# Gate broadcast, head squares and convolution steps of an mLSTM layer reordered and recast in a three-layer kernel

## The chip, the cores and the metric

One core of one Trainium2 chip runs the whole program in one launch. The metric is the device time of one execution in microseconds, as the median of several runs. TensorE (PE) multiplies, VectorE (DVE) and ScalarE (ACT) do the elementwise work, and SyncE (SP) issues the DMAs of the weights. GpSimd has almost nothing to do.

## The reference, cut to what matters

The kernel computes a block of multi-head latent attention, a block of mLSTM and a third block of mixed attentions with a large feed-forward part, for 256 tokens of width 2048 in float32. The change lies in the mLSTM block only. For each of its 8 heads (dk = 128, dv = 256), with `T` = 256 tokens:

```python
qk = silu(causal_depthwise_conv(x @ W_qk, w, b))       # 4 taps, 16 blocks of 128 rows
i, f = split(x @ W_g + gate_b)                         # 8 heads each
lf = log_sigmoid(f);  F = cumsum(lf)                   # over the tokens
a = i - F;            M = cummax(a)
D[s, t] = exp(a[s] - M[t])  for s <= t
A = (k^T q) * dk**-0.5 * D
h = (A^T v) / max(|sum_s A|, exp(-M - F))
h = rmsnorm(h) * head_norm;   out = (h * sigmoid(o) * silu(z)) @ W_out
```

The terms `-M[t]` and `-M[t] - F[t]` are one number per head and token. They have to stand in all 128 partitions before they can be added to a 128-row tile. That is the broadcast which the change is about.

## The kernel before

All activations live in on-chip memory, feature blocks of 128 rows by 256 tokens. The time goes into streaming the weights of all three layers. SyncE loads units of 1 MB, two halves of 1024 columns each (`raw`). Each half is split in two float32r parts whose sum is exact enough: ScalarE writes the high part (`hi`, L1471, into `WH`), and VectorE writes the rest (`lo`, L1965, into `WL`). Four such slots exist (`NW` = 4), so ScalarE may overwrite a slot once TensorE has finished the half that lay in it. A weight tile of 128 columns then costs TensorE a 512-column product with `WH` and a 256-column product with `WL` (`tile`, all through the helper at L1061). Half the tokens' result comes out through ScalarE (`second_half`, L1476) and VectorE adds the other half (`whole`, L1982).

The class `Plan` writes one list of steps per section of the program. Each engine walks through the same lists in order and does its own share of every step. Nothing is reordered at run time: an engine that waits in one step holds all that stands behind it. Between the steps of the recurrences, `pipe` puts weight tiles of the next projection (`filler`), so that TensorE has work.

Three places matter here.

- **Convolution.** The step `conv taps` n: ScalarE writes tap 0 with the bias into block n (L1648) and then does the SiLU of block n-1 (L1643). VectorE adds the other three taps (L2266, three instructions) as soon as ScalarE's tap 0 of the same n is there. Blocks 0 to 8 lie in the sections `conv` and `gates` up to the gate projection, blocks 9 to 15 among the tiles of the values projection (`vm`), whose outputs ScalarE copies out of PSUM (L1688).
- **Gates.** In the section `gates` VectorE computes `F`, `M` and the two broadcast rows on 8 partitions (L2302 to L2310). The result is `GR`, 8 x 512 float32. TensorE transposes `a` (L1244, L1245, step `gate turn`) and VectorE copies it (L2313).
- **The mLSTM pipeline.** `pipe` runs stages m0, m1, m3, m4, m5, m6, m7 over 8 heads, in each step in the order m5, m4, m3, m7, m1, m6, m0, head h being one step further in each stage. m0 is a product of one-hot rows `E8` (8 x 128 per head) with `GR` (8 x 512) in float32 into bank 3: every partition gets the two rows of its head. VectorE adds the mask (L2329, L2330), ScalarE takes the exponentials (L1714, L1715, L1718) and with L1718 frees bank 3 for the next m0. m3 (L2336) makes the weights, m4 is the product with the values. m5 on VectorE is denominator, reciprocal and cell (L2340, L2341, L2343, L2344), and on ScalarE the squares of the cell (L1723). m6 sums the squares on TensorE, m7 is the norm (L1480, L1481, L2351).

## Time and profile before

| | |
|---|---|
| median of 3 runs | 2044.36 us (2044.01 to 2045.74) |
| the profiled execution | 2044.31 us, its span in the trace 2042.8 us |
| TensorE busy | 2021.3 us, 99% of the span |
| VectorE, ScalarE busy | 1375.8 us (67%), 1052.9 us (52%) |
| mean granted TensorE clock | 0.998 |
| DMA | 356.41 MB, 174 GB/s on average |

The span is the time from the first to the last instruction that the profiler saw. The execution's own time has 1.5 us around it. A timeline row gives the start, the duration, the engine and line, then output and inputs with their shape, how many instructions the row merges, and in brackets how long the engine was idle before and what ended that. In a row that merges several, the duration is that of all of them together. Since the engines overlap the end of one instruction with the start of the next, the distance between two starts says what an instruction costs, and its duration is longer than that.

### The profile page before, as it was taken

Reading aid. Unit: us, or ns where it says so; the run is one execution under the profiler, and the core shown is the slowest. Engines: PE = TensorE matmul, PEld = TensorE weight load, DVE = VectorE, ACT = ScalarE, POOL = GpSimd, SP = SyncE. Lnnn points to the kernel's source line nnn. Section 1 sums busy time; section 2 is a strip of 40 time slices with the busy share of each in tenths; the row PEclk is TensorE's granted clock in tenths of the full one; section 3 lists DMA queues with packets and bytes.
Section 4 is the critical chain, followed back from the end, with each engine's and each line's share of the span. In section 5 each row is a group of like instructions: output and inputs, shape, how many; then the busy total and the mean of one; then the engine's idle time right before and its main releaser. Section 6 shows DMA issues by size and latency. Waiting matters only on the chain.

```text
span 2042.8 us, 29214 instructions
## 1 busy us (share of the span) xinstructions
PE 2021.3 (99%) x11592; PEld 1746.1 (85%) x11592; DVE 1375.8 (67%) x2130; ACT 1052.9 (52%) x1670; POOL 0.2 (0%) x4
## 2 busy tenths in 40 slices
PE   9999999999999999998999999999999999999999
PEld 7888878988878888897888888888888888888888
DVE  5656658986557776898467968576665556666554
ACT  5554445675445754575355755454444334444432
POOL 0000000000000000000000000000000000000000
PEclk9999999999999999999999999999999999999999
DMA  7554225454532355545544235555555555555552
GB/s 282 197 185 165 104 83 186 172 201 167 203 143 105 146 206 186 186 165 188 200 172 153 105 109 190 202 186 186 186 188 196 194 186 185 186 187 191 198 202 108
DMA packets 52807, 356.41 MB, mean 174 GB/s; under 512 B 5776, under 2 KB 9112, under 8 KB 10432
## 3 DMA queue, kind: packets, MB, share of 16 engines
q1 hardware_dynamic: 49872, 351.04, 47.5%
q10 hardware_dynamic: 2800, 3.50, 0.5%
q8 instruction: 92, 1.51, 0.3%
q14 instruction: 43, 0.35, 0.1%
HBM read 352.41 MB, written 2.11 MB: 174 GB/s over the span
## 4 chain that ended last, share of the span: by engine, by line
PE 87%; DVE 8%; ACT 2%; issue 1%; DMA 1%; SPq 0%; ACTq 0%; DVEq 0%
PE bank L1061 87%; DVE WL L1965 2%; ACT WH L1471 1%; DMA X<-in_x 1%; DVE AR L2343 0%; DVE AR L2128 0%; DMA mu_acc<-in_sgu 0%; DVE XP L2124 0%; DVE AR L1982 0%; PE bank L1199 0%; DVE AR L2241 0%; DVE AR L2238 0%; DVE AR L2117 0%; DVE AR L2407 0%; DVE AR L2344 0%
## 5 line engine op out<-in xcount | busy, mean ns | idle before, releaser
L1965 DVE TENSOR_TENSOR WL<-raw,WH 128x1024 fp32r<-128x1024 f32 x653 | 791.6, 1223 | 334.3 <-ACT WH L1471 325.7
L1471 ACT ACTIVATE WH<-raw 128x1024 fp32r<-128x1024 f32 x653 | 686.4, 1057 | 483.3 <-PE bank L1061 431.2
L1061 PE MATMUL bank<-XP,WH 128*128 128x512 f32 (+2 forms) x2096 | 670.6, 394 | 4.7 <-DVE WL L1965 4.1
L1061 PEld LDWEIGHTS bank<-XP,WL 128*128 128x128 f32 x2016 | 379.5, 188 | 83.4 <-DVE WL L1965 1.6
L1061 PE MATMUL bank<-FP,WH 128*128 128x512 f32 x1408 | 443.1, 395 | 0.0
L1061 PE MATMUL bank<-XP,WL 128*128 128x256 f32 (+1 forms) x2016 | 409.3, 279 | 1.3 <-DVE WL L1965 1.3
L1061 PEld LDWEIGHTS bank<-XP,WH 128*128 128x128 f32 (+1 forms) x2096 | 329.4, 188 | 18.7 <-issue 12.6
L1061 PEld LDWEIGHTS bank<-FP,WL 128*128 128x128 f32 x1408 | 264.5, 188 | 62.2
L1061 PE MATMUL bank<-FP,WL 128*128 128x256 f32 x1408 | 277.3, 278 | 0.0
L1061 PE MATMUL bank<-AP,WH 128*128 128x512 f32 x704 | 222.0, 395 | 0.0
L1061 PEld LDWEIGHTS bank<-FP,WH 128*128 128x128 f32 x1408 | 214.8, 189 | 0.4
L1476 ACT ACTIVATE AR<-bank 128x256 f32<-128x256 f32 x185 | 70.2, 382 | 243.7 <-PE bank L1061 243.5
L1982 DVE TENSOR_TENSOR AR<-bank,AR 128x256 f32<-128x256 f32 x185 | 77.8, 423 | 141.8 <-ACT AR L1476 141.5
L1061 PEld LDWEIGHTS bank<-AP,WL 128*128 128x128 f32 x704 | 132.3, 188 | 30.6
L1061 PE MATMUL bank<-AP,WL 128*128 128x256 f32 x704 | 139.6, 278 | 0.0
L1061 PE MATMUL bank<-WH,XP 128*128 128x512 f32 (+1 forms) x448 | 136.2, 380 | 3.4 <-DVE WL L1965 3.4
L1061 PE MATMUL bank<-AR 128*128 128x256 f32 (+6 forms) x512 | 107.9, 338 | 4.0 <-ACT AR L1718 1.7
L1061 PEld LDWEIGHTS bank<-AP,WH 128*128 128x128 f32 x704 | 107.9, 189 | 0.7
L1061 PEld LDWEIGHTS bank<-AR 128*128 128x128 f32 (+3 forms) x512 | 83.2, 188 | 23.9 <-issue 8.1
L1061 PEld LDWEIGHTS bank<-WH,XP 128*128 128x128 f32 x448 | 82.5, 188 | 19.2 <-DVE WL L1965 4.3
L1061 PE MATMUL bank<-WL,XP 128*128 128x512 f32 (+1 forms) x224 | 84.2, 376 | 0.0
L1061 PE MATMUL bank<-HP,WH 128*128 128x512 f32 x256 | 81.4, 396 | 0.4 <-DVE WL L1965 0.4
(310 smaller groups left out, 1750.7 us busy)
## 6 DMA issues: line engine op xcount, KB each, us to landing
raw<-in_W SPq DMA_DIRECT2D x330, 1024.0 KB, 4.8
out<-AR ACTq DMA_DIRECT2D x16, 128.0 KB, 2.0
X<-in_x SPq DMA_DIRECT2D x3, 512.0 KB, 10.3
raw<-in_W SPq DMA_DIRECT2D x2, 512.0 KB, 6.2
AR<-rv SPq DMA_DIRECT2D x1, 1024.0 KB, 5.1
cst<-in_cst ACTq DMA_DIRECT2D x1, 963.0 KB, 13.3
X<-in_x SPq DMA_DIRECT2D x2, 256.0 KB, 4.1
AR<-in_sgu SPq DMA_DIRECT2D x1, 512.0 KB, 5.7
```

The costliest lines, as they stand in the source:

```text
L1061: return pe.matmul(o, lhsT, rhs, start=start, stop=stop)
L1471: ac.activation(w_slot(WH, s), raw_half(hf), ACT.Copy).then_inc(s_hi, 1)
L1476: ac.activation(dst, bank[pl.bank_of[name, n, 0]][0:rows, T:2 * T], ACT.Copy).then_inc(s_half, 1)
L1965: tt(w_slot(WL, s), raw_half(pl.half_of[s]), w_slot(WH, s).bitcast(F32), ALU.subtract).then_inc(s_lo, 1)
L1982: tt(dst, psum(name, n)[0:rows, :], dst, ALU.add).then_inc(s_out["dve"], 1)
```

## The change

1. **Gate broadcast (m0).** `GR` is split in three bfloat16 parts that add up to it: VectorE casts, subtracts, casts, subtracts, casts (five new instructions on 8 x 512) into partitions 0, 32 and 64 of a zeroed tile `G3` (72 rows, one new memset). The one-hot rows are loaded on 72 rows instead of 8 and cast to bfloat16 once by ScalarE (`E3`). The product of a head is then one bfloat16 product of 72 rows, 512 columns.
2. **Head squares.** The ScalarE part of m5 becomes a step of its own, `m5 squares`, which stands behind m1 in each pipeline step instead of at m5's place. VectorE's part stays where it was.
3. **Convolution.** In `conv taps` n ScalarE does the SiLU of block n-2 first and then tap 0 of block n, and VectorE adds the taps of block n-1. There are therefore 18 such steps instead of 16 and one closing SiLU, and `gate table`, `gate exp`, `gate sums` and `gate turn` come two pieces of the values projection later (a piece is 4 tiles).

```diff
@@ -171,10 +171,11 @@
     put("tril", i[:, None] <= i[None, :])
     dist = 255 - np.arange(383)
     hot = (np.arange(32)[:, None] == rel_bucket(dist)[None, :]) & (dist >= 0)[None, :]
-    late = np.zeros((32, 766 + 1024), np.float32)
-    late[:, 0:383] = hot
+    late = np.zeros((72, 766 + 1024), np.float32)
+    late[0:32, 0:383] = hot
     late[0:8, 383:766] = np.where(dist >= 0, 0.0, NEG)
-    late[0:8, 766:] = np.repeat(np.eye(8), 128, axis=1)
+    for o in (0, 32, 64):
+        late[o:o + 8, 766:] = np.repeat(np.eye(8), 128, axis=1)
     r12 = np.zeros((64, 256))
     for m in range(128):
         r12[m % 32, m] = 1.0
@@ -359,8 +361,11 @@
                     k += shares[step]
                     go(filler, pieces * k // slots - done)
                     done = pieces * k // slots
+                what, s = (s[1], s[0]) if isinstance(s, tuple) else (None, s)
                 if 0 <= step - s < n:
-                    if callable(stages[s]):
+                    if what:
+                        self.say(what, step - s)
+                    elif callable(stages[s]):
                         stages[s](step - s)
                     else:
                         self.say(stages[s], step - s)
@@ -538,10 +543,9 @@
     go(p.proj(st["gates"]))
     p.big, p.turn = [0, 1, 2, 4], 0
     vp = p.proj_tm(st["vm"])
-    for n in range(9, 16):
+    for n in range(9, 18):
         say("conv taps", n)
         go(vp, 1)
-    say("conv end")
     say("gate table")
     go(vp, 1)
     say("gate exp")
@@ -555,7 +559,8 @@
     p.big = [0, 1]
     op, zp = p.proj(st["o"]), p.proj(st["mz"])
     fill = then(op, itertools.islice(zp, 4))
-    p.pipe(8, ["m0", "m1", "m3", "m4", "m5", "m6", "m7"], fill, 68, (1, 3, 4, 5), (4, 3, 2, 6, 1, 5, 0),
+    p.pipe(8, ["m0", "m1", "m3", "m4", "m5", "m6", "m7"], fill, 68, (1, 3, 4, 5),
+           (4, 3, 2, 6, 1, (4, "m5 squares"), 5, 0),
            [3] * 11 + [4] * 3)
     go(fill)
     p.big = [0, 1, 2]
@@ -867,7 +872,8 @@
 
 
         QK, Vm, O, HN = ar(0, 4096), ar(4096, 4096), ar(8192, 4096), ar(12288, 4096)
-        E8, GR = AR[0:8, 15360:16384], AR[0:8, 20992:21504]
+        E8, E3 = AR[0:72, 16384:17408], sb("E3", 1024, BF, at=a0_ + 4 * 15360)
+        GR, G3 = AR[0:8, 14848:15360], sb("G3", 512, BF, at=a0_ + 4 * 20992)
         ip, fp, ab, e1, lf, Fc, ai, Mx, one8 = (AR[0:8, 12544 + i * T:12544 + (i + 1) * T] for i in range(9))
         aT = small[:, 0:16]
         dk = float(128 ** -0.5)
@@ -973,7 +979,7 @@
 
         s_uh, s_ul, s_wn = sem("s_uh"), sem("s_ul"), sem("s_wn")
 
-        s_qk, s_gab, s_gexp, s_gr, s_gtt, s_aT = (sem("s_" + n) for n in ("qk", "gab", "gexp", "gr", "gtt", "aT"))
+        s_e3, s_qk, s_gab, s_gexp, s_gr, s_gtt, s_aT = (sem("s_" + n) for n in ("e3", "qk", "gab", "gexp", "gr", "gtt", "aT"))
 
 
         s_m0, s_m1, s_m2, s_m4, s_m3, s_m5, s_m6, s_m7c, s_m7, s_m8, s_m9, s_m10 = (
@@ -1251,8 +1257,8 @@
                 elif what == "m0":
                     take(3)
                     if h == 0:
-                        pe.wait_ge(s_e8, 16)
-                    mm(bank[3][:, 0:512], E8[:, 128 * h:128 * (h + 1)], GR, True, True).then_inc(s_m0, 1)
+                        pe.wait_ge(s_e3, 1)
+                    mm(bank[3][:, 0:512], E3[0:72, 128 * h:128 * (h + 1)], G3[0:72, :], True, True).then_inc(s_m0, 1)
                     free[3] = s_m4, h + 1
                 elif what == "m1":
                     take(4)
@@ -1644,11 +1650,12 @@
 
             def conv_taps(n):
 
-                ac.wait_ge(*outed("conv", n))
-                ac.activation(blk(QK, n), cs[n], ACT.Identity, scale=pcol("conv_w", 48 + n),
-                              bias=pcol("conv_b", n)).then_inc(s_tap, 1)
-                if n:
-                    conv_silu(n - 1)
+                if n >= 2:
+                    conv_silu(n - 2)
+                if n < 16:
+                    ac.wait_ge(*outed("conv", n))
+                    ac.activation(blk(QK, n), cs[n], ACT.Identity, scale=pcol("conv_w", 48 + n),
+                                  bias=pcol("conv_b", n)).then_inc(s_tap, 1)
 
             for what, n in pl.steps["conv"]:
                 if what == "hi":
@@ -1671,13 +1678,13 @@
                     hi(n)
                 elif what == "e8":
                     ac.wait_ge(*done("conv", AHEAD - 1))
-                    ac.dma_start(E8, dr["late"][0:8, 766:1790]).then_inc(s_e8, 16)
+                    ac.dma_start(E8, dr["late"][:, 766:1790]).then_inc(s_e8, 16)
                 elif what == "conv taps":
                     conv_taps(n)
-                elif what == "conv end":
-                    conv_silu(15)
                 elif what == "gate table":
                     exp_table()
+                    ac.wait_ge(s_e8, 16)
+                    ac.activation(E3[0:72, :], E8, ACT.Copy).then_inc(s_e3, 1)
                 elif what == "gate exp":
                     ac.wait_ge(s_gab, 1)
                     chain(ac.activation(e1, ab, ACT.Exp))
@@ -1716,7 +1723,7 @@
                     if h >= 4:
                         ac.wait_ge(s_m6, h - 3)
                     ac.activation(cap[h % 4], bank[3][:, 256:512], ACT.Exp).then_inc(s_m4, 1)
-                elif what == "m5":
+                elif what == "m5 squares":
                     ac.wait_ge(s_m7c, h + 1)
                     if h >= 2:
                         ac.wait_ge(s_m8, h - 1)
@@ -2260,6 +2267,9 @@
 
             def conv_taps(n):
 
+                n -= 1
+                if not 0 <= n < 16:
+                    return
                 y, c = blk(QK, n), cs[n]
                 dv.wait_ge(s_tap, n + 1)
                 for s in (1, 2, 3):
@@ -2298,6 +2308,7 @@
                     dv.wait_ge(*outed("gates", 0))
                 elif what == "gate exp":
                     stt(ab, fp, -1.0, fp, ALU.mult, ALU.min).then_inc(s_gab, 1)
+                    chain(dv.memset(G3[0:72, :], 0.0))
                 elif what == "gate sums":
                     chain(ts(lf, fp, 0.0, None, ALU.min))
                     dv.wait_ge(s_gexp, 1)
@@ -2307,7 +2318,12 @@
                     chain(tt(ai, ip, Fc, ALU.subtract))
                     chain(dv.tensor_tensor_scan(Mx, ai, ai, 0.0, ALU.max, ALU.max))
                     chain(ts(GR[:, 0:T], Mx, -1.0, None, ALU.mult))
-                    tt(GR[:, T:2 * T], GR[:, 0:T], Fc, ALU.subtract).then_inc(s_gr, 1)
+                    chain(tt(GR[:, T:2 * T], GR[:, 0:T], Fc, ALU.subtract))
+
+                    for o in (0, 32):
+                        chain(dv.tensor_copy(G3[o:o + 8, :], GR))
+                        chain(tt(GR, GR, G3[o:o + 8, :], ALU.subtract))
+                    dv.tensor_copy(G3[64:72, :], GR).then_inc(s_gr, 1)
                 elif what == "gate turn":
                     dv.wait_ge(s_gtt, 1)
                     dv.tensor_copy(aT, bank[5][:, 0:16]).then_inc(s_aT, 1)
```

Left out of it are only the hunk of a blank line and the one that loads 32 rows of `late` by name. Line numbers of the changed kernel are 6 to 16 higher in these parts: L1471 is L1477 there, L1476 L1482, L1688 L1695, L1697 to L1699 L1704 to L1706, L1714, L1715 and L1718 are L1721, L1722 and L1725, L1723 is L1730, L1648 L1657, L1643 L1649, L1965 L1972.

ScalarE in the mLSTM pipeline, from the exponentials of head 2 on (pipeline step 3), before (`s_ml_cell` is VectorE's cell being done, `s_ml_dec` its masked row):

```order
L1714 ACTIVATE AR_58<-AR_58,small_51 128x256 [waits s_ml_dec]
L1715 ACTIVATE AR_58<-AR_58,small_51 128x128
L1718 ACTIVATE AR_58<-bank3 128x256
L1471 ACTIVATE WH_56<-raw_55 128x1024 [waits s_proj,s_raw1]
L1723 ACTIVATE AR_58<-AR_58 128x512 [waits s_ml_cell]
L1471 ACTIVATE WH_56<-raw_55 128x1024 [waits s_proj,s_raw1]
L1476 ACTIVATE AR_58<-bank0 128x256 [waits s_proj]
L1697 ACTIVATE mu_acc_52<-AR_58 128x256 [waits s_olg,s_out_dve]
L1698 ACTIVATE mu_acc_52<-mu_acc_52 128x256 [waits s_achain]
L1699 ACTIVATE mu_acc_52<-mu_acc_52,cst_50 128x256 [waits s_achain]
```

The same place in the changed kernel:

```order
L1721 ACTIVATE AR_58<-AR_58,small_51 128x256 [waits s_ml_dec]
L1722 ACTIVATE AR_58<-AR_58,small_51 128x128
L1725 ACTIVATE AR_58<-bank3 128x256
L1477 ACTIVATE WH_56<-raw_55 128x1024 [waits s_proj,s_raw1] x2
L1482 ACTIVATE AR_58<-bank0 128x256 [waits s_proj]
L1704 ACTIVATE mu_acc_52<-AR_58 128x256 [waits s_olg,s_out_dve]
L1705 ACTIVATE mu_acc_52<-mu_acc_52 128x256 [waits s_achain]
L1706 ACTIVATE mu_acc_52<-mu_acc_52,cst_50 128x256 [waits s_achain]
L1721 ACTIVATE AR_58<-AR_58,small_51 128x256 [waits s_ml_dec]
L1722 ACTIVATE AR_58<-AR_58,small_51 128x128
L1725 ACTIVATE AR_58<-bank3 128x256
L1730 ACTIVATE AR_58<-AR_58 128x512 [waits s_ml_cell]
```

The squares (128x512) stood between two copies of weight halves, behind the exponentials of head 2. Now those two copies follow each other, and the squares of the same head come behind the exponentials of head 3, ahead of the two copies that follow.

ScalarE in the values projection, from the copies ahead of the first outputs (128x512) on, before (128x256 with `pv_49` is tap 0 of block 13, the one behind it the SiLU of block 12):

```order
L1471 ACTIVATE WH_56<-raw_55 128x1024 [waits s_proj,s_raw0] x2
L1688 ACTIVATE AR_58<-bank0 128x512 [waits s_proj]
L1688 ACTIVATE AR_58<-bank1 128x512 [waits s_proj]
L1648 ACTIVATE AR_58<-AR_58,pv_49 128x256 [waits s_out_dve]
L1643 ACTIVATE AR_58<-AR_58 128x256 [waits s_conv]
L1471 ACTIVATE WH_56<-raw_55 128x1024 [waits s_proj,s_raw1] x2
```

The same place in the changed kernel:

```order
L1477 ACTIVATE WH_56<-raw_55 128x1024 [waits s_proj,s_raw0] x2
L1695 ACTIVATE AR_58<-bank0 128x512 [waits s_proj]
L1695 ACTIVATE AR_58<-bank1 128x512 [waits s_proj]
L1649 ACTIVATE AR_58<-AR_58 128x256 [waits s_conv]
L1657 ACTIVATE AR_58<-AR_58,pv_49 128x256 [waits s_out_dve]
L1477 ACTIVATE WH_56<-raw_55 128x1024 [waits s_proj,s_raw1] x2
```

The SiLU (now of block 11) has moved ahead of tap 0 of block 13. VectorE's rows at this place read as before, but its taps there are now those of block 12, whose tap 0 stands one step earlier on ScalarE.

VectorE at the gate sums, from the second scan on, before:

```order
L2308 SCALAR_TENSOR_TENSOR AR_58<-AR_58 8x256 [waits s_vchain]
L2309 TENSOR_SCALAR AR_58<-AR_58 8x256 [waits s_vchain]
L2310 TENSOR_TENSOR AR_58<-AR_58 8x256 [waits s_vchain]
L1965 TENSOR_TENSOR WL_57<-raw_55,WH_56 128x1024 [waits s_hi] x4
L2313 COPY small_51<-bank5 128x16 [waits s_gtt]
```

The same place in the changed kernel:

```order
L2319 SCALAR_TENSOR_TENSOR AR_58<-AR_58 8x256 [waits s_vchain]
L2320 TENSOR_SCALAR AR_58<-AR_58 8x256 [waits s_vchain]
L2321 TENSOR_TENSOR AR_58<-AR_58 8x256 [waits s_vchain]
L2324 CAST G3_66<-AR_58 8x512 [waits s_vchain]
L2325 TENSOR_TENSOR AR_58<-AR_58,G3_66 8x512 [waits s_vchain]
L2324 CAST G3_66<-AR_58 8x512 [waits s_vchain]
L2325 TENSOR_TENSOR AR_58<-AR_58,G3_66 8x512 [waits s_vchain]
L2326 CAST G3_66<-AR_58 8x512 [waits s_vchain]
L1972 TENSOR_TENSOR WL_57<-raw_55,WH_56 128x1024 [waits s_hi] x4
L2329 COPY small_51<-bank5 128x16 [waits s_gtt]
```

Five instructions on 8 x 512 have come in ahead of the four weight halves and the copy of the transposed gates (128x16).

## Rows read from the trace of the kernel before

**Rows 1.** The page of the kernel before, its first part: engines, busy us, share, instructions

```profile
PE 2021.3 (99%) x11592; PEld 1746.1 (85%) x11592; DVE 1375.8 (67%) x2130; ACT 1052.9 (52%) x1670; POOL 0.2 (0%) x4
```

**Rows 2.** Waits of TensorE, 380 to 720 us: total us, times, longest us

```profile
PE bank L1061 <- ACT AR L1718: 1.7, 2, 1.3
...
PE bank L1061 <- issue: 0.4, 1, 0.4
PE bank L1061 <- DVE AR L1982: 0.3, 1, 0.3
```

**Rows 3.** Windows, TensorE: us, busy (count), granted clock, DMA share, GB/s

```profile
500.00:510.00 10.00, 8.36 (x37) 1.00 0.47 162
...
610.00:620.00 10.00, 8.75 (x38) 0.83 0.28 105
```

**Rows 4.** Timeline, TensorE, last gate broadcast and tiles behind it; columns: start us, us, instruction

```profile
646.72 1.12 PE L1061 MATMUL bank<-AR 8*128 8x512 f32 x2
647.77 0.50 PE L1061 MATMUL bank<-XP,WH 128*128 128x512 f32 x1
...
648.35 0.62 PE L1061 MATMUL bank<-XP,WH 128*128 128x512 f32 x2
...
649.04 0.63 PE L1061 MATMUL bank<-XP,WH 128*128 128x512 f32 x2
```

**Rows 5.** Timeline, ScalarE, the exponentials that free the bank for that broadcast

```profile
644.51 0.36 ACT L1718 ACTIVATE AR<-bank 128x256 f32<-128x256 f32 x1
```

**Rows 6.** Timeline, TensorE, a bf16 product of the MLA stage and what follows

```profile
182.99 0.23 PE L1061 MATMUL bank<-uv 1*128 1x128 bf16 x1
183.14 0.70 PE L1061 MATMUL bank<-QKN 128*128 128x256 f32 x2
```

**Rows 7.** Timeline, TensorE, values projection, about 502 us

```profile
501.99 0.39 PE L1061 MATMUL bank<-WH,XP 128*128 128x512 f32 x1
504.02 0.50 PE L1061 MATMUL bank<-WH,XP 128*128 128x512 f32 x1 [1.64 <-DVE WL L1965]
```

**Rows 8.** Timeline, ScalarE, the same stretch

```profile
500.67 0.60 ACT L1648 ACTIVATE AR<-AR,pv 128x256 f32<-128x256 f32 x1
```

**Rows 9.** Timeline, VectorE, the same stretch

```profile
501.30 1.52 DVE L2266 SCALAR_TENSOR_TENSOR AR<-AR,pv 128x255 f32<-128x255 f32 x3 [4.33 <-ACT AR L1648]
```

**Rows 10.** Timeline, TensorE, mLSTM steps 3 and 4 (gate broadcasts, weighted values)

```profile
600.58 1.12 PE L1061 MATMUL bank<-AR 8*128 8x512 f32 x2 [0.42 <-ACT AR L1718]
...
604.53 1.47 PE L1061 MATMUL bank<-AR 128*128 128x256 f32 x8
...
611.37 1.12 PE L1061 MATMUL bank<-AR 8*128 8x512 f32 x2 [1.25 <-ACT AR L1718]
...
616.88 1.47 PE L1061 MATMUL bank<-AR 128*128 128x256 f32 x8
```

**Rows 11.** Timeline, ScalarE, the same steps

```profile
606.07 0.63 ACT L1723 ACTIVATE AR<-AR 128x512 f32<-128x512 f32 x1 [4.60 <-DVE AR L2344]
606.61 1.04 ACT L1471 ACTIVATE WH<-raw 128x1024 fp32r<-128x1024 f32 x1
```

**Rows 12.** Timeline, VectorE, the same steps

```profile
603.10 0.42 DVE L2341 SCALAR_TENSOR_TENSOR AR<-bank,AR 128x256 f32<-128x256 f32 x1
...
605.35 0.69 DVE L2344 TENSOR_TENSOR AR<-bank,AR 128x512 f32<-128x512 f32 x1
...
607.68 1.23 DVE L1965 TENSOR_TENSOR WL<-raw,WH 128x1024 fp32r<-128x1024 f32 x1 [1.18 <-ACT WH L1471]
```

**Rows 13.** Timeline, VectorE, the gate sums and the copy behind the transposes

```profile
525.52 0.27 DVE L2304 MEMSET AR<- 8x256 f32 x1 [2.24 <-ACT AR L1684]
...
528.29 0.41 DVE L2310 TENSOR_TENSOR AR<-AR 8x256 f32<-8x256 f32 x1
...
532.74 1.23 DVE L1965 TENSOR_TENSOR WL<-raw,WH 128x1024 fp32r<-128x1024 f32 x1 [0.64 <-ACT WH L1471]
...
540.06 3.49 DVE L1965 TENSOR_TENSOR WL<-raw,WH 128x1024 fp32r<-128x1024 f32 x3
```

2 lines of the change are left out of this document (1 added, 1 removed).

## The prediction

> **What bounds the kernel now.** I read the page first, then the waits of TensorE, then the windows and the timelines of the stretches that the change touches. The page says that TensorE is busy for 2021.3 of 2042.8 us [rows 1]: nearly everything that another engine does is hidden, and time is only won where TensorE gets less to do or waits less. So each edit is read for two things: what it takes from TensorE's own stream, and which of TensorE's few waits it moves. Between 380 and 720 us, from the convolution to the end of the mLSTM pipeline, TensorE waits four times for more than a moment: 1.64 us for a low weight half [rows 7], 0.42 and 1.25 us for L1718, which frees the broadcast bank [rows 2, 10], and 0.4 and 0.3 us near the end of the pipeline [rows 2]. There is one thing more in the windows: from 610 to 620 us the granted clock is 0.83, while it is 1.00 around it [rows 3]. That is the lower of the two levels (1.2 GHz instead of 2.4) for about a third of those 10 us, right behind the 1.25 us wait and an 8-row product.
>
> **Part 1, the broadcast product.** Starts, not durations, price an instruction on TensorE. The last broadcast starts at 646.72 and the tile behind it at 647.77, so one costs 1.05 us; there are eight [rows 4]. Two weight tiles, 1536 columns, take 649.04 - 648.35 = 0.69 us, which is 0.45 ns a column [rows 4]. The only bfloat16 product of the trace with few rows takes 0.15 us from start to start for 128 columns [rows 6], of which 0.06 are columns and 0.09 a weight load that shows, because the number of rows changes. The new product has 512 columns: 0.23 + 0.09 = 0.32 us, a saving of 0.73 each. The floor is a product without that load (0.23, saving 0.82), the ceiling half of the old pair (0.52, saving 0.53); I take 0.73, since [rows 6] have the same kind of product between the same neighbours. The Trainium skill, TensorE: Matmul & The Clock Gate, section Back-to-back issue gap, gives 518 cycles for 512 columns, with nothing on top for a change of rows: 0.22 us, and by it the eight would save 6.6 us instead of 5.8. The trace has the added 0.09 us in [rows 6], and my sum goes by that.
>
> The saving counts in full where TensorE has no wait in front of its next broadcast. That is so for heads 0, 1, 2, 5, 6 and 7, where L1718 was done well before the broadcast that needs its bank; the closest is head 7, with L1718 over at 644.51 + 0.36 = 644.87 and the broadcast at 646.72 [rows 4, 5]. So 6 x 0.73 = **4.4 us**. Heads 3 and 4 come in part 2, because there a chain decides.
>
> VectorE pays for the split with five instructions on 8 x 512 and a memset. The nearest rows are 0.41 us for 8 x 256 and 0.69 us for 512 columns [rows 12, 13]; I take 0.5 for a cast and 0.73 from start to start for a subtraction, 3.0 us together (2.1 to 3.7). The block of the gate sums took 525.52 to 528.70 = 3.2 us [rows 13]. It now begins behind the low half that ended at 533.97 and ends near 533.97 + 0.2 + 3.2 + 3.0 = 540.3. The low half behind it then starts at about the time at which it started before, 540.06, held then by the transposes of the gates [rows 13], and TensorE didn't wait for it. There is room for more: TensorE ends the transposes at about 539.8 and has one half in front of the one in question, 12 products of 512 columns or 2.7 us, so it wants it at 542.5, and the half was done at 541.3. The block may grow by 1 us beyond my sum before it costs anything. ScalarE's new cast of 72 x 1024 costs about what a weight half costs, 1.04 us [rows 11], and ScalarE is idle for about half of the time; the table load is moved and not added; the load of E8 grows from 32 to 288 KB, less than a third of one of the 330 weight units, on ScalarE's own queue, and has several steps to land in. All of these: **0 us**. Moving `gate turn` two pieces later costs nothing either: its result is first read in the pipeline, after all of the values projection.
>
> **Part 2, the squares, and with them the broadcasts of heads 3 and 4.** ScalarE waits 4.60 us for VectorE's cell (L2344) before the squares at 606.07, and the copy of a weight half stands behind them and starts at 606.61 [rows 11]. VectorE, done at 606.50, waits 1.18 us for that copy before its low half at 607.68 [rows 12]. Behind it stand the output of a projection block, the masked row and the exponentials that free bank 3: this chain ends in TensorE's wait of 1.25 us at 611.37 [rows 10]. With the squares behind the exponentials, the copy is made long before, and the low half starts at 606.41 (two instructions of VectorE overlap by 0.09). The chain is 1.27 us shorter, so from broadcast 3 to broadcast 4 the time falls from 10.79 [rows 10] to 9.52 us. TensorE alone would want 10.79 - 1.33 (the wait counted by starts) - 0.73 = 8.73. So the chain still decides and a wait of 0.8 us stays: gain **1.3 us**.
>
> From broadcast 4 to the weighted values of head 2 it was 5.51 us, from broadcast 3 to those of head 1 3.95 [rows 10]. It is the same work, so the lower clock cost 1.56 us. I take it that the clock doesn't fall: a wait of 1.64 us at 502 us left it at 1.00 [rows 3, 7], the one here is down to 0.8, and the 8-row pair is gone. TensorE would then need 3.95 - 0.73 = 3.22 us. But there is a new wait: the squares (0.54 us, 606.07 to 606.61 [rows 11]) now stand in front of the copy that VectorE's low half and, behind it, the denominator L2341 need. That one ended 603.52 - 600.58 = 2.94 us behind broadcast 3 [rows 10, 12], so now 2.94 + 0.54 + 0.05 = 3.53. Gain 5.51 - 3.53 = **2.0 us**. In the other steps that copy isn't next in VectorE's line, or TensorE comes later by the same reckoning.
>
> Near the end of the pipeline two waits hang on the same pattern, ScalarE held by the cell with a weight half behind it: 0.4 and 0.3 us [rows 2], and about 0.16 more each by starts. Both should go: **1.0 us**.
>
> **Part 3, the convolution.** ScalarE makes tap 0 of block 13 behind two copies of values outputs, which wait for the end of their products, at 500.67 [rows 8]. VectorE has waited for that tap 4.33 us, until 501.30 [rows 9], with two low halves behind it, and TensorE waits from 501.99 to 504.02 [rows 7]. That is 2.03 us where 0.23 is usual, and 0.1 more at the next tile: 1.9 us. With VectorE one step behind, its tap 0 was made a step earlier, it doesn't wait, and the low halves are there: gain **1.9 us**. The SiLUs end two pieces later, still well before the pipeline reads them. What is late next: nothing that I find before the gate block of part 1.
>
> **Sum.** 4.4 + 1.3 + 2.0 + 1.0 + 1.9 = 10.6 us. The profiled execution took 2044.31 us (span and 1.5 around it), 0.05 less than the median of the runs: 2044.3 - 10.6 = **2033.7 us**.
>
> **Rivals.**
> - *The chain sets the pipeline.* If ScalarE and VectorE set the pace in all eight steps and not in one, the broadcasts of part 1 save nothing. What is left is 1.3 + 2.0 + 1.0 + 1.9 = 6.2: 2038.1 us. For it speaks the wait at head 3, which stays, and that VectorE goes from one instruction to the next in these steps; against it, that L1718 was 1.8 us or more ahead at the other heads [rows 4, 5]. 13 in 100.
> - *The clock falls all the same*, here or in another place where TensorE waits: 1.6 us of the gain come back, 2035.3 us. 8 in 100.
> - *The gate block holds TensorE.* The new instructions of VectorE take 3 us more than my sum, 2 us beyond the room there is, and the convolution's wait only moves to another low half (1.9 back): 2037.6 us; and if the change doesn't do what it says, the product costing what the old pair did (5.8 back), 2043.4. 5 in 100, most of it near the second.
> - *Slower: squares ahead of the weight copy.* The squares put 0.54 us in front of a weight half in each of eight steps. If each becomes a wait of TensorE and the clock falls each time (1.56 us), that costs 8 x 2.1 = 16.8 us against 1.9 + 5.8 + 1.0 = 8.7 that stay: 2052.4 us. It decides from six such steps on. Against it: the clock fell in one of the eight steps, the one with the longest wait. 2 in 100.
>
> My forecast has the other 72. A measurement of this kernel tells about 0.2%, 4.1 us, from no change. The forecast and the first two rivals are faster by more than that: 0.93; the third mostly is not: 0.05 within; 0.02 slower. The range: below, the floor of the product (0.7 us), the wait of head 3 gone (0.4) and another fall of the clock, of which the runs may have one more or less (1.6), reach 2031.0. Above, the ceiling of the product (1.6) gives 2035.3, and the chain rival 2038.1 is taken in: to 2038.5.
>
> **What would show it.** In the profile after: the product of `E3` and `G3` eight times, 0.3 us from start to start; no wait of TensorE at about 502 us and VectorE's taps without a wait for L1657; broadcast 4 behind broadcast 3 by 9.5 us with a wait under 1 us; granted clock 1.00 in the whole pipeline; a wait of about 0.3 us before the weighted values of head 2. Waits for L1725 at many heads would mean the first rival, a clock below 1.00 there the second, a wait for a low half near 540 us the third.

## The result, and the profile after

The changed kernel takes 2032.34 us (median of 5 runs, 2031.0 to 2037.08) beside 2044.36 us before (5 runs, 2043.31 to 2045.74): ratio 0.9952, 95% interval 0.9941 to 0.9962. The forecast of 2033.7 us lies 1.4 us above it. On another chip the same two kernels gave 2035.43 us (5 runs, 2031.11 to 2036.54) and 2042.42 us (9 runs, 2041.46 to 2043.9), ratio 0.9962, interval 0.9948 to 0.9975. So the kernel is faster by 0.4 to 0.5%, by 12.0 us on the first chip and 7.0 us on the second. Its runs spread more than those before: on the first chip three lie at 2031.0 to 2032.34 us and two at 2036.63 and 2037.08. The last section says what goes with that.

The profiled execution took 2032.34 us, span 2030.9 us, which is 11.9 us less than the span before. First the page of the changed kernel, part 1 (beside [rows 1]):

```profile
PE 2012.4 (99%) x11584; PEld 1744.9 (86%) x11584; DVE 1378.6 (68%) x2136; ACT 1054.1 (52%) x1671; POOL 0.2 (0%) x4
```

TensorE has 8 instructions less (one for each of eight head pairs) and 8.9 us less to do. Next the waits of TensorE in the changed kernel, from 380 to 720 us (beside [rows 2], which left out the one for a low half that [rows 7] show):

```profile
PE bank L1067 <- ACT AR L1725: 1.1, 2, 0.7
PE bank L1067 <- issue: 0.4, 1, 0.4
```

The wait of 1.64 us for a low half is gone, as are those at the end of the pipeline; L1725 (the old L1718) is waited for twice still. The 0.4 us put down to issue is at a new place, before the weighted values of head 2; the one of the same size before was near the end of the pipeline. The windows of TensorE (us, busy with count, granted clock, DMA share, GB/s) say the same of the clock (beside [rows 3]):

```profile
500.00:510.00 10.00, 10.00 (x46) 1.00 0.57 209
...
610.00:620.00 10.00, 10.00 (x59) 1.00 0.34 110
940.00:950.00 10.00, 7.51 (x34) 0.76 0.36 109
950.00:960.00 10.00, 10.00 (x57) 0.90 0.68 256
```

In the pipeline the clock stays at 1.00 in every 10 us from 380 to 720. At 940 to 960 us, behind waits that both kernels have there, it falls, as it did before the change at 960 to 970:

```profile
960.00:970.00 10.00, 8.95 (x49) 0.83 0.55 211
```

The timeline of TensorE in the changed kernel at the broadcasts of heads 3, 4 and 5 and the weighted values of heads 1 and 2 (beside [rows 4, 10]):

```profile
595.16 0.39 PE L1067 MATMUL bank<-G,E 72*128 72x512 bf16 x1 [0.42 <-ACT AR L1725]
...
598.20 1.54 PE L1067 MATMUL bank<-AR 128*128 128x256 f32 x8
...
604.57 0.39 PE L1067 MATMUL bank<-G,E 72*128 72x512 bf16 x1 [0.70 <-ACT AR L1725]
...
608.14 1.55 PE L1067 MATMUL bank<-AR 128*128 128x256 f32 x8 [0.38 <-issue]
...
615.02 1.03 PE L1067 MATMUL bank<-AR,cst 128*128 128x256 f32 x4
615.89 0.38 PE L1067 MATMUL bank<-G,E 72*128 72x512 bf16 x1
615.92 0.58 PE L1067 MATMUL bank<-XP,WH 128*128 128x512 f32 x1
616.34 0.40 PE L1067 MATMUL bank<-XP,WL 128*128 128x256 f32 x2
```

From broadcast 3 to 4 it is 9.41 us (10.79 before), from broadcast 4 to the weighted values of head 2 it is 3.57 us (5.51 before). The starts at 615.89 and 615.92 say nothing of the price of a broadcast: 0.03 us can't hold 512 columns. So I measure across it, from the head sums in front to the first low product behind: 616.34 - 615.02 = 1.32 us. Before it was 2.35, from these two rows of the kernel before:

```profile
645.76 1.03 PE L1061 MATMUL bank<-AR,cst 128*128 128x256 f32 x4
...
648.11 0.40 PE L1061 MATMUL bank<-XP,WL 128*128 128x256 f32 x2
```

That is 1.03 us less, where 0.73 was forecast. ScalarE and VectorE in the changed kernel in the same step (beside [rows 11, 12]), ScalarE first:

```profile
603.45 0.51 ACT L1721 ACTIVATE AR<-AR,small 128x256 f32<-128x256 f32 x1 [3.38 <-DVE AR L2346]
...
604.15 0.36 ACT L1725 ACTIVATE AR<-bank 128x256 f32<-128x256 f32 x1
604.42 0.62 ACT L1730 ACTIVATE AR<-AR 128x512 f32<-128x512 f32 x1
604.94 2.00 ACT L1477 ACTIVATE WH<-raw 128x1024 fp32r<-128x1024 f32 x2
```

```profile
606.02 1.23 DVE L1972 TENSOR_TENSOR WL<-raw,WH 128x1024 fp32r<-128x1024 f32 x1 [2.61 <-ACT WH L1477]
...
607.61 0.42 DVE L2357 SCALAR_TENSOR_TENSOR AR<-bank,AR 128x256 f32<-128x256 f32 x1
```

ScalarE goes from the exponentials to the squares without a wait; the long wait is now before the exponentials, for the masked row. The copy stands behind the squares, and VectorE waits 2.61 us for it; the denominator (L2341 before, L2357 now) ends at 608.03, 3.46 us behind the broadcast, and the weighted values come 0.11 us later.

Where the time went, from the starts of TensorE's first instruction at each place (before, after, in us; the profiled executions):

| place | before | after | gain since the row above |
|---|---|---|---|
| first convolution product | 381.17 | 380.78 | 0.4 (no part of the change) |
| broadcast, head 0 | 572.85 | 570.39 | 2.1 |
| head 1, 2, 3 | 581.74, 589.23, 600.58 | 578.26, 584.73, 595.16 | 1.0, 1.0, 0.9 |
| head 4 | 611.37 | 604.57 | 1.4 |
| head 5 | 624.66 | 615.89 | 2.0 |
| head 6, 7 | 634.99, 646.72 | 625.19, 635.89 | 1.0, 1.0 |
| mLSTM output projection | 788.73 | 775.34 | 2.6 |
| group norm's projection | 1211.43 | 1199.46 | -1.4 |
| FFN | 1303.81 | 1291.85 | 0.0 |

The gain up to the output projection is 13.4 us, and 1.4 us come back between it and the group norm's projection. Instruction by instruction, 0.3 to 0.4 of them are lost by about 965 us (952 after), where the clock falls in both kernels and further in the changed one. The other 1.1 are lost at L2626 (L2642 after): at 1117 us (1104 after) only the changed kernel waits for it, at 1131 us (1119 after) both do, and behind it stands a transfer. VectorE, the first rows before and the second after, at the scaling of the gating matrix:

```profile
1111.06 1.23 DVE L2580 TENSOR_TENSOR AR<-AR,cst 128x1024 f32<-128x1024 f32 x1 [0.91 <-DMA mu_acc<-in_sgu]
```

```profile
1099.10 1.23 DVE L2596 TENSOR_TENSOR AR<-AR,cst 128x1024 f32<-128x1024 f32 x1 [1.94 <-DMA mu_acc<-in_sgu]
```

The last load of the spatial gate is issued at 1105.22 before and at 1092.12 after, and VectorE starts 5.8 and 7.0 us later. Behind it TensorE waits 1.2 us before, and 0.6 and 1.4 us after.

### The profile page after: what moved, and what is told of

It is laid out like the page before. It is cut to its first block, busy times and chain, and to the rows that moved or that the text cites. A ratio compares the mean times of both kernels' runs of the same rounds, so it can differ in the third digit from the quotient of the medians.

```text
span 2030.9 us, 29206 instructions
## 1 busy us (share of the span) xinstructions
PE 2012.4 (99%) x11584; PEld 1744.9 (86%) x11584; DVE 1378.6 (68%) x2136; ACT 1054.1 (52%) x1671; POOL 0.2 (0%) x4
## 4 chain that ended last, share of the span: by engine, by line
PE 90%; DVE 6%; ACT 2%; DMA 1%; issue 1%; SPq 0%; ACTq 0%; DVEq 0%
PE bank L1067 89%; DVE WL L1972 2%; DMA X<-in_x 1%; ACT WH L1477 1%; DVE AR L2135 0%; DMA mu_acc<-in_sgu 0%; DVE XP L2131 0%; PE bank L1205 0%; DVE AR L2248 0%; DVE AR L2245 0%; DVE AR L2124 0%; DVE AR L2423 0%; DVE AR L2159 0%; DVE AR L2611 0%; DVE AR L1989 0%
## 5 line engine op out<-in xcount | busy, mean ns | idle before, releaser
L1972 DVE TENSOR_TENSOR WL<-raw,WH 128x1024 fp32r<-128x1024 f32 x653 | 792.0, 1223 | 338.0 <-ACT WH L1477 329.3
L1477 ACT ACTIVATE WH<-raw 128x1024 fp32r<-128x1024 f32 x653 | 686.5, 1057 | 480.2 <-PE bank L1067 427.9
L1067 PEld LDWEIGHTS bank<-XP,WH 128*128 128x128 f32 (+1 forms) x2096 | 329.0, 188 | 10.6 <-issue 5.4
L1482 ACT ACTIVATE AR<-bank 128x256 f32<-128x256 f32 x185 | 70.2, 383 | 252.2 <-PE bank L1067 252.1
L1067 PE MATMUL bank<-AR 128*128 128x256 f32 (+4 forms) x496 | 99.1, 329 | 3.0 <-DVE AR L2642 2.0
L1067 PEld LDWEIGHTS bank<-AR 128*128 128x128 f32 (+2 forms) x496 | 80.7, 189 | 20.7 <-issue 6.0
```

The costliest lines, as they stand in the source:

```text
L1067: return pe.matmul(o, lhsT, rhs, start=start, stop=stop)
L1477: ac.activation(w_slot(WH, s), raw_half(hf), ACT.Copy).then_inc(s_hi, 1)
L1482: ac.activation(dst, bank[pl.bank_of[name, n, 0]][0:rows, T:2 * T], ACT.Copy).then_inc(s_half, 1)
L1972: tt(w_slot(WL, s), raw_half(pl.half_of[s]), w_slot(WH, s).bitcast(F32), ALU.subtract).then_inc(s_lo, 1)
```

## The experiments

Twelve runs, four to a chip: the first four stood beside 2042.1 us for the kernel before (1 run), the next four beside 2043.74 (7 runs, 2042.4 to 2045.53), the last four beside 2042.42 (9 runs). Of those with one run, what counts is the profile.

**The convolution's part alone.** The kernel before with

```diff
-    for n in range(9, 16):
+    for n in range(9, 18):
         say("conv taps", n)
...
-                ac.wait_ge(*outed("conv", n))
...
-                if n:
-                    conv_silu(n - 1)
+                if n >= 2:
+                    conv_silu(n - 2)
+                if n < 16:
+                    ac.wait_ge(*outed("conv", n))
```

and VectorE's taps one block behind.

> The kernel before with part 3 alone (ScalarE's SiLU two blocks behind, VectorE's taps one block behind, gate steps two pieces later). My theory: TensorE's wait for a low half at about 502 us goes and nothing else changes; the first gate broadcast, at 572.85 us before, starts 1.9 to 2.1 us earlier, and all from there to the end of the pipeline keeps that distance: broadcasts 3 and 4 still 10.8 us apart, with waits of 0.42 and 1.25 us. Rival: the wait only moves to another low half, and the first broadcast starts less than 0.5 us earlier. Clock: if the fall behind broadcast 4 belongs to the wait and the 8-row pair, it stays; if it hangs on where the stretch lies in time, it can move or go. About 2042 us.

2039.46 us. The convolution and the values projection take 189.70 us from the first product to broadcast 0 (191.68 before), a gain of 2.0, and the wait for a low half is gone. What I had not reckoned with is that the granted clock stays at 1.00 in 600 to 620 us. TensorE of this kernel (columns as in the timeline above):

```profile
608.25 1.12 PE L1060 MATMUL bank<-AR 8*128 8x512 f32 x2 [1.25 <-ACT AR L1716]
...
612.20 1.03 PE L1060 MATMUL bank<-AR 128*128 128x256 f32 x5
```

The wait of 1.25 us and the 8-row pair are those of [rows 10], and yet the weighted values come 3.95 us behind the broadcast, not 5.51. So this wait and this pair together are not enough to bring the clock down.

**The squares alone.** The kernel before with

```diff
-    p.pipe(8, ["m0", "m1", "m3", "m4", "m5", "m6", "m7"], fill, 68, (1, 3, 4, 5), (4, 3, 2, 6, 1, 5, 0),
+    p.pipe(8, ["m0", "m1", "m3", "m4", "m5", "m6", "m7"], fill, 68, (1, 3, 4, 5),
+           (4, 3, 2, 6, 1, (4, "m5 squares"), 5, 0),
```

and ScalarE's `m5` renamed.

> The kernel before with part 2 alone (head squares behind the exponentials). My theory, a chain over ScalarE and VectorE: broadcasts 3 and 4 are 9.5 us apart instead of 10.79, the wait before broadcast 4 falls from 1.25 to about 0.1 us, the clock doesn't fall behind it, so the weighted values of head 2 come 3.95 us behind it instead of 5.51; the waits of 0.4 and 0.3 us near the end go. Together 3.8 us, with the 8-row float32 pairs still in place, about 2040.5 us. Rival: the chain goes on past the squares (another wait holds VectorE's low half), and broadcasts 3 and 4 stay 10.8 us apart. Second rival on the clock: the 8-row pair alone lets it fall; then 5.5 us stay between broadcast 4 and the weighted values of head 2.

2039.23 us. From broadcast 3 to 4 it takes 9.47 us, with no wait of TensorE ahead of broadcast 4:

```profile
600.21 1.12 PE L1065 MATMUL bank<-AR 8*128 8x512 f32 x2 [0.41 <-ACT AR L1722]
...
609.68 1.12 PE L1065 MATMUL bank<-AR 8*128 8x512 f32 x2
...
613.63 1.47 PE L1065 MATMUL bank<-AR 128*128 128x256 f32 x8
```

The whole wait of 1.25 us (1.32 by starts) is gone, the weighted values of head 2 are at 613.63, 3.95 us behind, and the waits at the pipeline's end are gone too. From the first convolution product to the output projection it gains 4.6 us, 1.56 of it the clock.

**The product alone.** The changed kernel with the convolution and the squares put back:

```diff
-           (4, 3, 2, 6, 1, (4, "m5 squares"), 5, 0),
+           (4, 3, 2, 6, 1, 5, 0),
...
-    for n in range(9, 18):
+    for n in range(9, 16):
         say("conv taps", n)
         go(vp, 1)
+    say("conv end")
```

> The kernel before with part 1 alone (bf16 product of three parts; squares ahead of the weight copy and gate steps where they were). My theory: a broadcast costs 1.02 us less wherever TensorE doesn't wait, as in the changed kernel, so 6 us over heads 0, 1, 2, 5, 6, 7; broadcasts 3 and 4 stay 10.8 us apart, since the chain decides, and the wait before broadcast 4 grows from 1.25 to about 2.3 us. In the gate block VectorE is 2.7 us longer at a place where it had 1.8 us of room, so TensorE gets a new wait of about 0.9 us for a low half at about 531 us. Clock: if the 8-row pair had a share in the fall, it doesn't fall (weighted values of head 2 about 3.0 us behind broadcast 4); if a long wait is enough, it falls as before or more (over 4 us). About 2037 us without the fall, 2038.5 with it.

2041.55 us, 3 us above the upper of the two times expected. Its TensorE has a new wait, at the gate block:

```profile
532.46 0.50 PE L1067 MATMUL bank<-WH,XP 128*128 128x512 f32 x1 [1.24 <-DVE WL L1973]
```

Its windows of 600 to 620 us:

```profile
600.00:610.00 10.00, 7.92 (x46) 0.97 0.14 52
610.00:620.00 10.00, 10.00 (x53) 0.86 0.23 74
```

Where TensorE doesn't wait, the broadcasts stand 7.87 and 6.47 us apart (8.89 and 7.49 before), 1.02 less each. But from broadcast 3 to 4 it stays at 10.78, with a wait of 2.08 us: that interval belongs to the chain of VectorE and ScalarE, and the product only lengthens the wait in it. Behind that wait the weighted values of head 2 come 4.54 us after the broadcast, where the version without any wait (mask early, below) has 3.02: the clock fell here too, though the product has 72 rows. So the 8-row pair isn't needed for a fall. Near the pipeline's end a wait of 1.14 us appears, and one of 1.24 us at the gate block. The gain from the first convolution product to the output projection is 4.5 us, of the 8.2 that eight times 1.02 would be. The three parts alone gain 3.6, 4.6 and 4.5 us over this stretch, and the 1.56 us of the clock fall is in both of the first two sums. Counted once, they make 11.2 us; all at once it is 13.0. What made the time longer than expected lies further on: 2.1 us come back between the output projection and the group norm's projection (424.79 us against 422.69 before), with a clock of 0.54 at 950 to 960 us among them. The product needs the other two parts to be worth its price, one to shorten the chain, the other to move the gate block.

**One of the three parts.** The changed kernel with

```diff
-                    mm(bank[3][:, 0:512], E3[0:72, 128 * h:128 * (h + 1)], G3[0:72, :], True, True).then_inc(s_m0, 1)
+                    mm(bank[3][:, 0:512], E3[0:8, 128 * h:128 * (h + 1)], G3[0:8, :], True, True).then_inc(s_m0, 1)
```

It broadcasts the highest part of the gates alone and leaves the other two out.

> The changed kernel with the broadcast product on the 8 rows of the largest part alone; the two smaller parts are left out of it. It asks why the new product costs 0.23 us and not 0.32. Theory A: a weight load shows when the product uses few rows of the array, whatever the type; then, from the start of the four products of head sums in front of the last broadcast to the low product of the tile behind it, the distance is 1.5 us or more (1.32 in the changed kernel with 72 rows, 2.35 in the kernel before). Theory B: a bf16 load is hidden whatever the rows; then it stays 1.32 us. Nothing else should change, about 2032 us or, by A, 1 to 1.6 us more.

2034.21 us, nominally slower than the full product, though it multiplies 8 rows and not 72. TensorE of this kernel at the last of the free broadcasts:

```profile
615.98 1.03 PE L1067 MATMUL bank<-AR,cst 128*128 128x256 f32 x4
616.94 0.39 PE L1067 MATMUL bank<-G,E 8*128 8x512 bf16 x1
617.25 0.51 PE L1067 MATMUL bank<-XP,WH 128*128 128x512 f32 x1
617.59 0.40 PE L1067 MATMUL bank<-XP,WL 128*128 128x256 f32 x2
```

Across the broadcast it takes 1.61 us, 0.29 more than with 72 rows, and 0.31 us from its start to the next: the size of the forecast's 0.32, though the forecast meant it for 72 rows. Up to the output projection, this kernel loses 1.65 us to the changed one (396.21 against 394.56 us from the first convolution product).

**The float32 product on 72 rows.** The kernel before with E8 loaded on 72 rows and the gate rows read on 72, the added ones zero:

```diff
-        E8, GR = AR[0:8, 15360:16384], AR[0:8, 20992:21504]
+        E8, GR = AR[0:72, 15360:16384], AR[0:8, 20992:21504]
+        GRW = AR[0:72, 20992:21504]
...
-                    mm(bank[3][:, 0:512], E8[:, 128 * h:128 * (h + 1)], GR, True, True).then_inc(s_m0, 1)
+                    mm(bank[3][:, 0:512], E8[:, 128 * h:128 * (h + 1)], GRW, True, True).then_inc(s_m0, 1)
```

> The kernel before, its float32 broadcast product on 72 rows instead of 8 (64 of them zero), everything else in place. It asks how much of the 1.02 us per broadcast comes from the number of rows and how much from the type. Theory A (loads show on few rows): from the start of the four products of head sums in front of the last broadcast to the low product of the tile behind it 2.35 us become about 1.95 to 2.05, the four passes of 512 columns staying. Theory B (rows don't matter): 2.35 us as before. Clock: if 8 active rows had a share in the fall behind broadcast 4, it goes here; if the wait alone decides, it stays at a wait of 1.25 us or more.

2040.68 us. Its TensorE at the last broadcast:

```profile
642.06 1.03 PE L1062 MATMUL bank<-AR,cst 128*128 128x256 f32 x4
642.92 1.02 PE L1062 MATMUL bank<-AR 72*128 72x512 f32 x2
...
644.03 0.40 PE L1062 MATMUL bank<-XP,WL 128*128 128x256 f32 x2
```

1.97 us across it against 2.35 on 8 rows. So the saving of 1.03 has two parts that can be made separately: from the float32 pair to one bfloat16 product it is 2.35 - 1.61 = 0.74 us on 8 rows and 1.97 - 1.32 = 0.65 on 72; from 8 rows to 72 it is 0.38 in float32 and 0.29 in bfloat16. The 0.65 are nearly three times the 0.23 us of 512 columns, so the pair costs about four times the bfloat16 product, not twice. TensorE's weight loads show where the second part lies. The kernel before, weight loads at broadcast 0:

```profile
572.85 0.29 PEld L1061 LDWEIGHTS bank<-AR 8*128 8x128 f32 x2 [0.25 <-issue]
573.90 0.19 PEld L1061 LDWEIGHTS bank<-XP,WH 128*128 128x128 f32 x1 [0.76 <-issue]
```

and with 72 rows:

```profile
572.53 0.42 PEld L1062 LDWEIGHTS bank<-AR 72*128 72x128 f32 x2
573.19 0.19 PEld L1062 LDWEIGHTS bank<-XP,WH 128*128 128x128 f32 x1 [0.24 <-issue]
```

The load on 8 rows starts with its own product at 572.85, and the load behind it starts only when the pair is over; the load on 72 rows starts ahead, while the product in front still runs (its pair starts at 572.76), and the next follows sooner. At all eight broadcasts on 8 rows, in either type, the load starts with its product; in float32 on 72 rows it starts 0.21 to 0.23 us ahead at the six that no wait precedes. In the changed kernel the records are less plain: the load starts 0.21 to 0.22 us ahead at heads 5 to 7 and with its product at the others, and nothing is exposed at either.

This run also bears on the clock. TensorE waits 1.43 us before broadcast 4, longer than in the kernel before, and the wait for a low half at 502 us is there too, and yet the clock stays up:

```profile
610.00:620.00 10.00, 9.80 (x54) 1.00 0.23 86
```

**A longer gate block.** The changed kernel with 12 more casts of 8 x 512 ahead of the split, which write what the split then writes over:

```diff
+                    for _ in range(REPEAT):
+                        chain(dv.tensor_copy(G3[0:8, :], GR))
                     for o in (0, 32):
```

with `REPEAT = 12`.

> The changed kernel with twelve more casts of 8 x 512 (0.45 us each from start to start, 5.4 us in all) at the head of the split. It measures the room in the gate block. My theory: VectorE's low half behind the block ends 1.2 to 1.3 us before TensorE wants it, so TensorE waits about 4.1 us at about 541 us and the first broadcast starts about 4.1 us later than in the changed kernel (570.39 us). Rival: the room is much larger, because other low halves lie ahead, and TensorE waits less than 2 us.

2039.42 us. VectorE and TensorE of this kernel:

```profile
534.46 5.36 DVE L2325 CAST G<-AR 8x512 bf16<-8x512 f32 x12
```

```profile
543.90 0.79 PE L1068 MATMUL bank<-WH,XP 128*128 128x512 f32 x1 [4.50 <-DVE WL L1973]
```

Of 5.4 us (12 casts, 0.45 from start to start), 4.50 came out as a wait, so the block of the changed kernel had 0.9 us of room, near the 1 us of the forecast. Behind the wait the granted clock is 0.66 in 540 to 550 us, and broadcast 0 comes 7.3 us later than in the changed kernel, counted from the first convolution product. So an edit here that looks free is on the edge.

**The squares one place later, and the mask early.** Two versions of the changed kernel that follow from the chain of the step:

```diff
-           (4, 3, 2, 6, 1, (4, "m5 squares"), 5, 0),
+           (4, 3, 2, 6, 1, 5, (4, "m5 squares"), 0),
```

> The changed kernel with the squares one place further back, behind the weight halves that stand ahead of m6. My theory: the wait of 0.38 us before the weighted values of head 2 goes, since the squares (0.52 us) no longer stand in front of the copy that VectorE needs; the wait of 0.70 us before broadcast 4 stays, since no squares stand in that chain. 0.4 to 0.5 us less, not to be told from the changed kernel by time alone. Rival: the sums m6 wait for the later squares, and the time is the same or longer.

2032.06 us (median of 4, 2031.05 to 2036.19; ratio 0.9949, interval 0.9932 to 0.9966). The wait of 0.38 us before the weighted values of head 2 is gone, and they come 3.04 us behind the broadcast: what held them was the weight copy behind the squares, as forecast. From broadcast 0 to the output projection it takes 204.39 us (204.95 in the changed kernel).

```diff
-           (4, 3, 2, 6, 1, (4, "m5 squares"), 5, 0),
+           (4, 3, 2, (1, "m1 mask"), 6, 1, 5, (4, "m5 squares"), 0),
```

with VectorE's masked row and ScalarE's exponentials as a step `m1 mask` of their own.

> squares_later's place moved on: the changed kernel with the squares behind m6 and VectorE's mask and ScalarE's exponentials directly behind m3, before the weight halves and the output of the projection block. My theory: bank 3 is freed 2 us or more earlier, so the waits before broadcasts 3 and 4 (0.42 and 0.70 us) go as well, and the pipeline holds TensorE nowhere: 1.5 to 1.9 us less than the changed kernel. Rival: ScalarE now waits for VectorE's mask with weight copies behind it, and TensorE waits for low halves instead: the same or slower.

2033.56 us (median of 4, 2031.16 to 2036.09). The trace lists no wait of TensorE at all from 380 to 720 us; broadcast 4 comes 8.45 us behind broadcast 3, and the pipeline takes 202.72 us. But its profile has a clock of 0.66 in 1000 to 1010 us, and the time was no better. So I ran it again, with the changed kernel on the same chip:

> The changed kernel with the mask's product ahead of the other parts of a step and the squares one place later, unaltered from its first run, where it stood at 2033.56 us (2031.16 to 2036.09) with a granted clock of 0.63 to 0.86 in three stretches behind the pipeline. From the first broadcast of the pipeline to the output projection's first product it took 202.72 us, the changed kernel 204.95. Theory A, these 2.2 us reach the end: 2029.5 to 2030.5 us where no stretch behind falls further than in the changed kernel. Theory B, they are given back at the waits and the clock falls between 880 and 1210 us, as 1.5 us of the change's own gain were: 2031 to 2033 us, no difference from the changed kernel.

> The changed kernel, unaltered, on the same chip as the version with the mask early, so that the two can be told apart. 2031 to 2033 us, and a pipeline of 204.9 to 205.0 us from its first broadcast to the output projection. If chance sets the clock falls, its profile shows the granted clock at 940 to 960 us at other values than 0.76 and 0.90, and the medians of the two versions lie within 1 us of each other.

With the mask early 2030.01 us (5 runs, 2029.6 to 2034.43; ratio 0.9945, interval 0.9932 to 0.9957), the changed kernel 2035.43 us (2031.11 to 2036.54; ratio 0.9962, interval 0.9948 to 0.9975). I had expected 2031 to 2033 us for the changed kernel. The intervals overlap, and over all runs, of two chips each, the medians are 2032.71 us (9 runs) and 2034.41 us (10 runs). The pipeline again takes 202.72 us, 2.2 less than 204.90; of this 0.7 come back before the group norm's projection. The version is the best of those run, by 1.5 us at most in what the traces share, and I can't tell that difference in the times. In the profile of the changed kernel from this chip the clock fell less at 940 to 960 us (0.87 and 0.96) and at another place as well:

```profile
1200.00:1210.00 10.00, 7.99 (x38) 0.84 0.24 86
```

There the first profile has 1.00 behind the same wait of 2.0 us, and from the group norm's projection to the FFN it takes 93.92 us here and 92.39 there.

**The clock fall once more.** The kernel before and the convolution's part alone, unaltered:

> The kernel before, unaltered, for a second profile on another execution. In its first profile the granted clock is 0.83 in the 10 us from 610 and head 2's weighted values come 5.51 us behind the broadcast product of head 4; where one part of the change was made alone, with the same wait of 1.25 us ahead of that broadcast, the clock stayed at 1.00 and they came 3.95 us behind. Theory A, the fall belongs to this kernel's work there (the wait, the two passes on 8 rows and the loads): it recurs, 5.3 to 5.6 us. Theory B, the fall hangs on chance, the phase of the chip against the kernel: 3.9 to 4.0 us and a clock of 1.00 here, or a fall of another size. Time 2041 to 2046 us.

> The convolution's part alone, unaltered from its first run, for a second profile. Theory A, the absence of a clock fall in 610 to 620 belongs to this kernel: head 2's weighted values come 3.9 to 4.0 us behind the broadcast product of head 4 again. Theory B, chance: the fall may show here (up to 5.5 us) or not. Either way the fall near 950 is there, of a size between 0.5 and 0.9 in a window of 10 us. Time 2038 to 2042 us.

2042.82 and 2041.35 us. The kernel before, TensorE at broadcast 4 and the weighted values of head 2, and its window:

```profile
610.04 1.12 PE L1061 MATMUL bank<-AR 8*128 8x512 f32 x2 [1.23 <-ACT AR L1718]
...
615.54 1.47 PE L1061 MATMUL bank<-AR 128*128 128x256 f32 x8
```

```profile
610.00:620.00 10.00, 9.96 (x45) 0.83 0.23 83
```

and with the convolution's part:

```profile
610.22 1.12 PE L1060 MATMUL bank<-AR 8*128 8x512 f32 x2 [1.23 <-ACT AR L1716]
...
614.16 1.47 PE L1060 MATMUL bank<-AR 128*128 128x256 f32 x8
```

```profile
610.00:620.00 10.00, 9.79 (x53) 1.00 0.25 89
```

The weighted values of head 2 come 5.50 and 3.94 us behind broadcast 4 (5.51 and 3.95 in the first profiles). The fall recurs in the one kernel and is absent again in the other, at start times that differ by 1.3 and 2.0 us from those of the first profiles. So, as far as two profiles of each can tell, it isn't drawn anew in each execution, though the instructions and the wait around it are the same in both kernels. The place in time doesn't decide either: 610.04 us goes with a fall and 610.22 us with none. Nor is it enough that TensorE waits at 502 us, as it does in the first kernel and not in the second: float32 on 72 rows has that wait and no fall.

## Why the prediction was right

The time lies within the forecast's range, and the steps of the forecast are the places where time was won. That it came within 1.4 us is partly luck: up to the output projection the gain is 13.0 us and not 10.6 (without the 0.4 us ahead of the change), 1.7 us of the difference from one mis-sized term, and a loss of 1.4 us behind it, which was not in the sum, took more than half of the excess back. The time on the second chip lies in the range as well, though the gain there was only 7.0 us. Its profile (2033.39 us) shows 1.5 us lost where the clock falls at 1200 us, for which the sum had no term; its slower runs have no profile. By its steps, to be compared with the table above:

- **TensorE's own work and its waits decide:** held. Every gain and loss is at a place where TensorE lost an instruction or a wait.
- **The price of a broadcast, 0.73 us saved:** this term was mis-sized. It is 1.03 where no wait stands ahead, above even the 0.82 that I called the most; for the six heads the sum is 6.1 us and not 4.4. Two steps failed. The larger is "starts, not durations, price an instruction": start to start the old pair takes 1.05 us, but its 8-row loads also delay the neighbours on both sides, which comes to about 0.2 us that only the distance across it holds. The smaller is "a weight load that shows, because the number of rows changes", 0.09 us, taken from a product on 1 row [rows 6]. The number of rows changes with 72 rows too, and no load shows; it is the few rows that matter, 0.29 us on 8. The rule of the Trainium skill, TensorE: Matmul & The Clock Gate, section Back-to-back issue gap, that I had set against [rows 6] was nearer for 72 rows: its 518 cycles make, by an estimate, a saving of 0.83 (1.05 less 0.22). The rows show 1.03, and the rest is what the old pair costs its neighbours. My sign of 0.3 us from start to start didn't show either: the starts are 0.03 us apart.
- **Squares, broadcast 3 to 4:** forecast 9.52 us with a wait of 0.8, measured 9.41 with 0.70. Held: the product alone left the interval at 10.78, the squares alone took it to 9.47. That the chain and not TensorE decides there was the point on which the price of this term hung.
- **Squares, broadcast 4 to the weighted values:** forecast 3.53 us, measured 3.57, with a new wait of 0.38 (forecast 0.3). The place and its size held, and putting the squares one later removed it. The denominator ended 3.46 us behind the broadcast (608.03 - 604.57), which is the 3.53 of the reckoning less 0.07.
- **The clock doesn't fall:** came true, its reason didn't. I gave the shorter wait and the missing pair as grounds. The convolution's part alone kept the wait and the pair and had no fall in either profile; float32 on 72 rows had none behind 1.43 us; the product alone had one behind 2.08 us without the pair. So the length of the wait from 1.2 to 1.4 us doesn't settle it and the pair isn't needed. Whether a wait of 0.7 us can bring a fall, and what does set it, is open; that this term of 1.56 us came true was in part luck.
- **End of the pipeline:** forecast 1.0, measured 1.5 (2.6 less the 1.0 of the last broadcast). Mis-sized in the same direction as the price of the pair.
- **Convolution:** forecast 1.9, measured 2.1 (2.0 with this part alone). My sign that VectorE's taps would not wait for L1657 failed: it still waits for tap 0, 2.25 us instead of 4.33, but its low halves come in time.
- **The gate block, 0:** held in sum, and its room as well (0.9 us measured, 1 forecast). The reckoning of five instructions, 3.0 us, stands beside 2.74 (535.12 to 537.86 in the rows below). It is free only together with the convolution's part: without it the block stands two pieces earlier, and TensorE waits 1.24 us. VectorE of the changed kernel (beside [rows 13]):

```profile
535.12 0.41 DVE L2324 CAST G<-AR 8x512 bf16<-8x512 f32 x1
535.57 0.68 DVE L2325 TENSOR_TENSOR AR<-AR,G 8x512 f32<-8x512 f32 x1
...
537.44 0.42 DVE L2326 CAST G<-AR 8x512 bf16<-8x512 f32 x1
```

- **Not in the sum:** -1.4 us behind the output projection, about 1.1 of it at the spatial gate. VectorE starts 7.0 to 7.5 us after the issue of the last of the spatial gate's loads in every kernel with the bfloat16 product, and 5.4 to 5.8 in those without; with float32 on 72 rows it is 6.1. So the loss goes with the product's part, and not with how early the kernel gets there (the convolution's part alone gets there 4.6 us earlier, with 5.6 us and no loss). Why the load lands later isn't known. The larger table of constants isn't enough: float32 on 72 rows has the same table and the same load of E8, and loses 0.1 us there. What is left is what only the kernels with the bfloat16 product have, the split, the cast of E8 and the product itself, and no run took these apart.
- **Rivals.** The chain as the pace of all eight steps is refuted by the 1.02 us at six heads; that it sets the pace at head 3 was in the forecast. The clock fell elsewhere in some runs of the changed kernel (0.84 at 1200 us), which is the second rival in small. Squares ahead of the copy cost one wait of 0.38 us in one step of eight.

## What to carry to other kernels

Price a small product by the distance between fixed neighbours on either side of it, not by its own start and the next: what it costs its neighbours lies outside it, here 0.2 us beside 1.05. Where an interval is set by a chain of other engines, taking work from TensorE there only lengthens the wait, so first ask which of the eight repeats of a step is that interval, and shorten the chain together with the product. And an edit that is free beside its partners can cost without them: the five small instructions of VectorE have 0.9 us to spare where they stand, and are 1.24 us too long two pieces earlier.

## What the runs showed of the hardware

- A product on 8 rows costs TensorE more than one on 72 rows of the same columns: 0.38 us more as a float32 pair, 0.29 us more in bfloat16. The weight load on 8 rows begins with its product (572.85 us both), that of the float32 product on 72 rows 0.23 us ahead of it (572.53 and 572.76). Which number of rows begins to be pulled ahead wasn't tried.
- The same wait of 1.25 us, followed by the same products, goes with a granted clock of 0.83 in one kernel (two profiles) and of 1.00 in another that differs only 60 us and more ahead of it (two profiles). A wait of 1.43 us goes with 1.00 in a third kernel, one of 2.08 us with 0.97 and 0.86 in a fourth (one profile each).
- In the later stages the fall varies between executions of one kernel: 1.00 or 0.84 in the changed kernel at 1200 us, with 1.5 us more in that stage. Its ten runs reach from 2031.0 to 2037.08 us, and their mean clock from 0.999 to 0.996. By an estimate from these, 0.003 of 2031 us is 6.1 us, which is the size of that spread; where the clock fell in the slower runs isn't known, since they have no profile.
